# Delta rule of a hybrid decoder step: substitution, decays, samples' norm and late reciprocals in another order, with products of ones in the first group

## What is computed

```python
diff = gam[..., :, None] - gam[..., None, :]          # gam: cumulated gates
decay = where(incl, exp(diff), 0)
a_mat = where(strict, beta * (k @ k.T) * decay, 0)
tinv = triangular_solve(eye + a_mat, eye)             # inverse of a unit lower triangle
value = tinv @ (v * beta);  kcum = tinv @ (k * beta * exp(gam))
qk = (q @ k.T) * decay
# over the chunks, with state s:
u = value - kcum @ s
o = (q * exp(gam)) @ s + qk @ u
s = s * exp(gam_last) + (k * exp(gam_last - gam)).T @ u
# then
o = o * rsqrt(mean(o * o) + eps) * norm_w * silu(z)   # z: a projection of the layer's input
```

## Time and profile before

| | |
|---|---|
| median of 3 runs | 2327.48 us (2322.49 to 2330.67) |
| profiled execution | 2326.65 us, span 2324.8 us |
| TensorE busy, mean granted clock | 2173.9 us (94%), 0.969 |
| VectorE, ScalarE, GpSimd busy | 1005.6, 577.4, 1123.5 us |
| delta rule stage | 1238 to 1748 us of the span |

### The profile page before, as it was taken

The page is one execution under the profiler, slowest core; times in us unless marked ns, Lnnn a source line. Parts: engine busy times, 40 slices in busy tenths (PEclk is TensorE's granted clock), DMA queues, the critical chain, the costliest instruction groups (busy, mean ns, idle before and its releaser), DMA issues. The chain is left out here.

```text
span 2324.8 us, 33108 instructions
## 1 busy us (share of the span) xinstructions
PE 2173.9 (94%) x12562; PEld 1621.2 (70%) x12562; DVE 1005.6 (43%) x1879; ACT 577.4 (25%) x1292; POOL 1123.5 (48%) x1075
## 2 busy tenths in 40 slices
PE   9898999899999999899996798888899999999997
PEld 6675555477777777677775667675767767777776
DVE  5343675435411341467884634343443163313422
ACT  2103677410000000155553324242420010000011
POOL 3212555357653564565783524334227276644653
PEclk9999999999999999999997899989999999999998
DMA  9725002722222211512223223242303122122211
GB/s 330 221 81 179 1 2 84 285 73 73 73 73 89 75 55 74 195 55 70 71 76 80 55 63 120 50 131 55 123 24 131 73 89 74 55 75 107 73 73 41
DMA packets 125911, 216.46 MB, mean 93 GB/s; under 512 B 73602, under 2 KB 96002, under 8 KB 109762
## 3 DMA queue, kind: packets, MB, share of 16 engines
q1 hardware_dynamic: 119234, 197.13, 25.5%
q0 software_dynamic: 3088, 14.03, 1.8%
q10 hardware_dynamic: 3440, 3.25, 0.4%
HBM read 185.08 MB, written 37.55 MB: 96 GB/s over the span
## 5 line engine op out<-in xcount | busy, mean ns | idle before, releaser
L2014 PE MATMUL ps<-xn,ring 128*128 128x288 f32 x768 | 198.8, 407 | 5.4 <-DVE xn L2117 3.2
L2014 PE MATMUL ps<-hid,ring 128*128 128x288 f32 x768 | 192.8, 406 | 0.0
L2014 PEld LDWEIGHTS ps<-xn,ring 128*128 128x128 f32 x768 | 145.3, 190 | 48.3 <-DVE xn L2117 5.9
L2014 PEld LDWEIGHTS ps<-hid,ring 128*128 128x128 f32 x768 | 145.6, 190 | 40.7 <-ACT p L2051 0.8
L2097 POOL TENSOR_TENSOR prod<-prod,rstd 128x1152 f32<-128x1152 f32 x32 | 84.0, 2623 | 179.5 <-DVE prod L2181 163.2
L2051 ACT ACTIVATE p<-ps 128x288 f32<-128x288 f32 x48 | 19.7, 411 | 597.4 <-PE ps L2014 597.4
L3725 PE MATMUL ps<-xn,ring 128*128 128x288 f32 x512 | 146.3, 425 | 5.7 <-PE ps L3823 4.0
L2014 PE MATMUL ps<-x_sum,wsum 128*128 128x288 f32 x512 | 130.6, 407 | 3.4 <-DVE x_sum L2121 1.9
L1122 POOL TENSOR_SCALAR ring<-ring,fac 128x128 f32<-128x128 f32 (+2 forms) x96 | 92.4, 980 | 83.1 <-DVE fac L1551 83.1
L2071 POOL TENSOR_TENSOR wsum<-ring 128x512 f32<-128x512 f32 x64 | 81.9, 1280 | 99.4 <-DMA ring<-in_w_mlp 91.5
L2014 PE MATMUL ps<-hid_sum,wsum 128*128 128x288 f32 x512 | 128.4, 407 | 0.1
(11 more groups left out here) (597 smaller groups left out, 4643.7 us busy)
## 6 DMA issues: line engine op xcount, KB each, us to landing
ring<-in_w_mlp SPq DMA_DIRECT2D x64, 1024.0 KB, 4.8
ring<-in_w_gdn_in SPq DMA_DIRECT2D x16, 1024.0 KB, 4.9
ring<-in_w_nsa_in SPq DMA_DIRECT2D x9, 1024.0 KB, 17.5
ring<-in_w_gdn_z SPq DMA_DIRECT2D x8, 1024.0 KB, 5.2
x<-in_seq_state SPq DMA_DIRECT2D x4, 2048.0 KB
out_seq_state<-x SPq DMA_DIRECT2D x4, 2048.0 KB, 11.6
ring<-in_w_gdn_out SPq DMA_DIRECT2D x8, 1024.0 KB, 5.6
out_win_old<-in_win_rows POOLq DMA_DIRECT2D x1, 8064.0 KB, 46.5
```

The lines of the kernel that those rows point to most:

```text
L2014: mm = nc.tensor.matmul(S.ps[:, base + BANK[p], 0:HT], stationary(p, blk.units[pair // 4], pair % 4), moving(blk.kind, p, pair), start=pai ...
```

## The change

- **VectorE**: chunks 12 and 13 get their unit length before the first keys step of group 0; 15 stays behind tile 2; 14 goes into the samples' part of group 0. The samples' norm of each group is made in its own samples' part.
- **ScalarE**: in group 0, decay 1 follows values and keys of tile 0. In other groups the decays of tiles 0 and 1 are made at the end of the group before, as are the square, root and output of the samples' norm.
- **GpSimd**: three of the eight scalings of the projection's input go before the first gaps, five behind the first two tiles. The samples' front goes before the substitution. The gaps and grown keys of the next group's tiles 1 and 0 go between the substitution and the scaling of the states.
- **TensorE**: in group 0, products of ones (128 x 512 outputs, `keep_busy`) where later groups have fillers: 6, 2, 1, 1 and one behind each of the last four steps of the first `join`, fourteen by the code. The key products for the next group's inverses go behind the value product of tile 0. The samples' norm is turned in its own group. One filler of the samples' front moves one step later.
- **SP**: the next group's rows and grown rows are loaded before the inverses are stored, its inverses after the ring load; the key products are stored after the loads for tile 3.
- The substitution's working tiles go from `root2` to `rstd` (free once 13 is made), gates to `shared`, keys to a free part of a tile in set 1.

```diff
-LATE_AT = {(0, -1): 12, (0, 0): 13, (0, 1): 14, (0, 2): 15}
+LATE_ORDER = (12, 13, 15, 14)
...
-        place = BlockPlace(S.root2[:, 0:256], S.root2[:, 256:512], S.root2[:, 512:576], S.rstd[:, 0, 0:32], S.rstd[:, 0, 32:288])
+        place = BlockPlace(S.rstd[:, 0, 0:256], S.rstd[:, 0, 256:512], S.rstd[:, 0, 512:576],
+                           S.shared[:, SMALL_AT + 24:SMALL_AT + 56], wide[1]["t"][:, 256:512])
...
                 if hg < 3:
+                    nxt = [tile(hg + 1, i) for i in range(2)]
+                    wait_step(sp, C[1], "pe", w[3].job, "out")
+                    rows_load(nxt[1])
+                    grown_load(nxt[1])
+                    wait_step(sp, Q, "pe", hg, "p4")
+                    rows_load(nxt[0])
...
                     block_inverses_out(sp, blocks, place, hg + 1)
                 sp.wait_ge(zd.product, 4 * hg + 2)
...
+                ring_load(2 * hg + 4)
+                if hg < 3:
+                    sp.wait_ge(blocks.stored, 256 * (hg + 2))
+                    wait_step(sp, Q, "pe", hg, "value")
+                    for x in nxt:
+                        t_load(x)
+                        inverse_load(x)
...
+            scaled(0, 3)
+            for i in range(2):
+                decay_gaps(tile(0, i))
+                grown_keys(tile(0, i))
+            scaled(3, KD)
...
                 seq_rows(hg)
+                seq_front(hg)
                 for _ in substitution:
                     pass
-                seq_front(hg)
+                if hg < 3:
+                    for i in (1, 0):
+                        decay_gaps(tile(hg + 1, i))
+                        grown_keys(tile(hg + 1, i))
                 wait_step(pool, Q, "pe", hg, "value")
...
+                def pause(n, ones):
+                    if hg:
+                        fill(n, left)
+                    else:
+                        keep_busy(S, ones, 7)
+
                 first_products(first)
-                fill(1, left)
+                pause(1, 6)
                 keys_turned(first)
-                fill(2, left)
+                pause(2, 2)
                 joins = join(first)
                 next(joins)
-                fill(1, left)
+                pause(1, 1)
                 first_products(second)
                 next(joins)
                 keys_turned(second)
-                fill(1, left)
+                pause(1, 1)
                 for _ in joins:
-                    fill(1, left)
+                    pause(1, 1)
...
+                    if i == 0 and hg < 3:
+                        pe.wait_ge(z_out, 4 * hg)
...
-                    fill((1, 3, 0, 1, 1, 1, 1, 1)[k])
+                    fill((1, 2, 1, 1, 1, 1, 1, 1)[k])
...
                 pe.sem_inc(Q.sem["pe"], 1)
+                turn(NQ, 0, hg)
                 fill(2)
...
-                decay(w[0])
-                decay(w[1])
+                if hg == 0:
+                    decay(w[0])
                 values(w[0])
                 late_keys(w[0])
+                if hg == 0:
+                    decay(w[1])
                 values(w[1])
-                if hg:
-                    square(*norm_of(hg, -1), hg - 1, PT)
...
+                square(*norm_of(hg, PT), hg, PT)
+                root(*norm_of(hg, PT))
+                if hg < 3:
+                    for i in (1, 0):
+                        decay(tile(hg + 1, i))
+                silu_z(hg, 1)
+                out(*norm_of(hg, PT), hg, PT)
+                silu_z(hg, 2)
...
+                if hg == 0:
+                    unit_length(12)
+                    unit_length(13)
                 keys(w[0])
...
                 by_sequence(0)
+                if hg == 0:
+                    unit_length(14)
+                last = norm_sum(*norm_of(hg, PT))
+                next(last)
                 for j in range(4):
                     if j < 3:
                         by_sequence(j + 1)
+                    if j == 1:
+                        next(last)
```

More of the change, by code:

```diff
@@ L3328, in _ @@
                 else:
[L3329 to L3337, removed]
                     sp.wait_ge(zd.product, 4 * hg)
-                    unit = 2 * hg + 3
-                    nxt, unit = (zd, unit) if unit < 8 else (out_d, unit - 8)
-                    sp.dma_start(S.ring[:, unit % SLOTS], nxt.weights[unit]).then_inc(nxt.loaded[unit % SLOTS], 16)
+                    ring_load(2 * hg + 3)
                     sp.wait_ge(seq_add, hg * 8)
@@ L3459, in _, with scaled @@
                 pool.sem_inc(c.sem["pool"], len(c.order["pool"]))
[L3460 to L3463, removed]
+            def scaled(first, last):
+                for k in range(first, last):
+                    g.tensor_tensor(S.xn[:, k], S.xn[:, k], S.rstd[:, 1], ALU.mult).then_inc(xn_ready, 1)
+            scaled(0, 3)
[3 more added lines that the diff above has]
+            scaled(3, KD)
             g.memset(zm, 0.0).then_inc(zm_zero, 1)
@@ L3466, in _ @@
                 substitution = block_inverses(pool, S, place, hg + 1) if hg < 3 else iter(())
-                decay_gaps(tile(hg, 2))
-                grown_keys(tile(hg, 2))
-                if hg == 0:
-                    for k in range(KD):
-                        g.tensor_tensor(S.xn[:, k], S.xn[:, k], S.rstd[:, 1], ALU.mult).then_inc(xn_ready, 1)
-                decay_gaps(tile(hg, 3))
-                grown_keys(tile(hg, 3))
+                for i in range(2, 4):
+                    decay_gaps(tile(hg, i))
+                    grown_keys(tile(hg, i))
                 if hg:
@@ L3485, in _ @@
                     g.tensor_tensor(seq_state[:, j], seq_state[:, j], seq_total(S, hg, j), ALU.mult).then_inc(seq_decayed, 1)
-                if hg < 3:
-                    for i in range(2):
-                        decay_gaps(tile(hg + 1, i))
-                        grown_keys(tile(hg + 1, i))
             last_gate()
@@ L3933, in _ @@
                 for i in range(PT):
-                    last = norm_before(hg, i)
+                    last = norm_before(hg, i) if i else None
                     if w[i + 1]:
@@ L3946, in _ @@
                     if last:
[L3947 removed]
+                        out(*last, hg, i - 1)
                     if w[i + 1]:
@@ L3972, in _ @@
                 act.sem_inc(Q.sem["act"], 1)
-                if hg == 3:
-                    square(*norm_of(3, PT), 3, PT)
-                    root(*norm_of(3, PT))
-                for c in range(1, 4 if hg == 3 else 3):
-                    if c == 3:
-                        out(*norm_of(3, PT), 3, PT)
-                    silu_z(hg, c)
+                square(*norm_of(hg, PT), hg, PT)
[6 more added lines that the diff above has]
+                silu_z(hg, 2)
+                if hg == 3:
+                    silu_z(hg, 3)
         @block.vector
@@ L4172, in _ @@
                 by_sequence(0)
-                last = norm_sum(*norm_of(3, PT)) if hg == 3 else iter(())
-                next(last, None)
+                if hg == 0:
+                    unit_length(14)
+                last = norm_sum(*norm_of(hg, PT))
+                next(last)
                 for j in range(4):
@@ L4183, in _ @@
                                         ALU.add).then_inc(seq_add, 1)
-                for _ in last:
-                    pass
 def gdn_out_stage(S, block):
```

46 lines of the change are left out of this document (18 added, 28 removed).

## The result

The changed kernel takes **2309.35 us** (median of 5 runs, 2303.71 to 2311.1) against 2323.77 us of the kernel before on the same chip (5 runs, 2322.49 to 2330.67): a ratio of 0.9928, with a 95% interval of 0.9906 to 0.995. It is faster, by 14 us where 37 were forecast. The profiled execution took 2311.1 us (span 2309.4, mean granted clock 0.974).

The account below looks back on a forecast made before the run. TensorE's instruction order, its waits for other engines' order and low clock behind them bound the stage; group 0 -15.5, groups 1 and 2 -9.1 each, group 3 -3.6, together -37.3 us, gave 2290 us, range 2278 to 2309.

Parts of the forecast that it names:

- Reciprocals 13 and 14 leave the loop: Group 0's tile loop: TensorE's waits of 4.79 and 4.09 us and the low clock behind them go, 12.5 us gained.
- Substitution behind the samples' front: Samples' part of groups 1 and 2: the 4.18 us wait for GpSimd goes and the clock recovers, 7.0 us each.
- A filler moved: Samples' part of all four groups: a filler set in a 0.51 us wait gives 0.5 us each.
- Start of group 0: Earlier values and keys steps, and products of ones holding the clock, gain 4 us; bounds +1 and -6.
- Reciprocal 14: Samples' part of group 0: 4.5 us on VectorE costs nothing, covered by GpSimd's delay; without cover some 2 us, once.
- GpSimd late: Samples' part of groups 0 to 2: GpSimd's later state scalings delay the second update product, +1.5 us each.
- Group starts: Groups 1 to 3: moved norm, earlier decays and recovered clock save 3.1 us per group.
- the 3.44 us wait: Group 0's tile loop: the wait for reciprocal 15, kept in tile 2, stays as the one such wait left.
- the wait of 4.18 us: Samples' part of groups 1 and 2: TensorE's wait for GpSimd, still in the substitution, would be gone.
- The clock gives nothing back: Rival, chance 0.18: remaining waits keep TensorE's clock low, some 18 us of gain is missing, 2308 us.
- GpSimd bounds the samples' part: Rival, chance 0.12: VectorE holds up GpSimd's instructions, whose chain ends 6 us later in three groups, 2308 us.
- More comes back: Rival, chance 0.10: the clock holds through the start and all group starts, some 8 us more, 2282 us.

Follow-up runs that it names:

- e7: Changed kernel with the four late reciprocals (12 to 15) back where they were before the change; 2313.49 us, 0.9951 of the kernel before.
- e5: Changed kernel with GpSimd making the samples' front behind the substitution again; 2321.06 us, 0.9977 of the kernel before.
- e6: Changed kernel with all eight gate input scalings on GpSimd behind the first two tiles' gaps and grown keys; 2304.68 us, 0.9915 of the kernel before.
- e8: Changed kernel with tile 2's rows before weights and states, state scalings before next gaps, reciprocal 14 after group 0's last state addition, gate inputs scaled late; 2273.66 us.
- e1: Changed kernel without its fourteen products of ones in group 0's start; 2307.16 us, 0.9915 of the kernel before.
- e2: Changed kernel with reciprocal 14 behind group 0's last state addition instead of before the second spread; 2301.66 us, 0.9884 of the kernel before.
- e4: Changed kernel with GpSimd scaling the samples' states ahead of the next group's gaps and grown keys; 2300.72 us, 0.989 of the kernel before.
- e3: Changed kernel with SP issuing tile 2's rows and ready inverses before the weights and sample states; 2286.44 us, 0.9822 of the kernel before.
- e9: Kernel before, with only tile 2's rows issued by SP before the weights and states; 2311.94 us, 0.9935 of the kernel before.
- e10: Changed kernel with early tile 2 rows, early state scalings, late reciprocal 14 and late gate input scalings, but no products of ones; 2278.97 us, 0.978.

## Why the prediction was wrong

The direction and most of the mechanism were right, the size was not: 2290 forecast, 2309 measured, 0.35 us beyond the range. By its steps:

- *Reciprocals 13 and 14 leave the loop*, -12.5: right; -15.5 measured, of which 12.2 by e7. Waits and clock both came back.
- *Substitution behind the samples' front*, -7.0: right, -6.9 and -7.0 by e5. *A filler moved*, -0.5: -0.4 in group 3.
- *Start of group 0*, -4: **failed**, +0.3. The step that failed is "the keys step ends at 1247.9, the first inverse product can start at 1248.0", 9.9 us after the stage's start; it started 12.1 after. It priced each late chunk at 4.5 us, from a trace in which nothing of GpSimd ran beside the multiply, though the change puts GpSimd's scalings there: the two chunks took 10.9 us, not 9. The products behind the wait then ran at the low clock. e6 has a start 3.5 us shorter, e8 2.3. I had cited the rule of the shared port (the Trainium skill, SBUF — State Buffer) against the change, but charged it only in the samples' part; by the rows 1.62 and 1.84 us beside GpSimd against 1.00 and 0.76, that rule and the trace agree here too. The ones were worth 0.9 us in the start and 3.2 in the group by e1, at twice the price assumed for one.
- *Reciprocal 14*, nothing, "GpSimd's delay covers it; without cover some 2 us": **failed**, 4.5 by e2. It ends, multiply and all, at 1349.5, and behind it stand two steps of the norm and a spread of 2.35 us before the first addition. I had moved one instruction and not the queue behind it; the clock then doubled the price.
- *GpSimd late*, +1.5: the mechanism was right. In group 0 it measured 1.6 (e8 against e2), in groups 1 and 2 3.1 and 3.0 (e4), because there the wait of 0.9 us was followed by a filler at the low clock.
- *Group starts*, -3.1 each: **failed**, and for more than the lost 4.6 us. The step was "the product runs in the wait and the following one waits instead: I take 1.2 us". It put the 2.94 us down to the norm's place in ScalarE's order and counted the late rows as something unmoved, when it was the rows that ended last: their distance from the group's start is the same 29.9 us, so nearly nothing could be gained in front of them: the wait that I had put at 1.2 us is 4.9, 5.6 and 5.3. The clock of 0.64 behind it stayed too (L3576 took 1.02 us against 0.67 in e3). e3 and e9 show it.

Of the misses, 4.3 us are the start, 4.8 the samples' part of group 0, 3.6 those of groups 1 and 2, 4.6 the group starts, 1.8 the norm's turn, which moved from the next group's loop to behind the last update; the loop gave 3.0 more than forecast. That is 16.1 of the 16.2 us between -37.3 and -21.1.

Of the signs named, the 3.44 us wait stayed in the loop, the wait of 4.18 us was gone, and a new wait stood before the second update; but group 0 was not some 120 us long, and the samples' part took 45.8, 42.7, 42.7 and 39.6 us, not 41.

Two rivals named 2308 and so came nearest. "The clock gives nothing back" did so for another reason than the true one: the clock did come back where the waits went (group 0 from 0.83 to 0.93). "GpSimd bounds the samples' part" was true in small: 1.6 us in group 0 and 3 in groups 1 and 2, not 6 in three. "More comes back" (2282) did not come true either: e3 comes near its number (2286) because a wait went. No wait of TensorE was for a load of inverses, and the 0.95 for faster was justified.

Open: what the attention part's clock depends on, the gap of 2.5 us of e10, why a filler behind a wait of 0.9 us ran at the low clock in some executions and not in others, and the 2.06 us for the copy at L3864, which stayed in every kernel with the change. None was tried. Nor were the moves at the group starts (the norm, the decays a group ahead, the block keys, SP's order) undone one by one, so their -0.8, -2.7 and -1.2 us are shown as a sum only.

## What to carry to other kernels

When a wait is put down to a copy on an in-order engine, ask what that engine itself was waiting for just before; if that is a load, look at what stands ahead of the load in its queue before you rearrange any compute. Here the place of two loads in one queue gave 21 us, and 16 in the kernel before, three quarters of what all the moves of the change gave. When an instruction is moved onto an engine with slack, price it with its neighbours: what stands behind it on the queue, and the other engine that will be running beside it.

## What the runs showed that was not expected

- The clock was low behind a wait of only 0.89 us between two updates: the filler behind it took 3.76 us in place of 2.18, with a clock of 0.76 in the window from 1475 to 1482 us:

```profile
1475.00:1482.00 7.00, 6.41 (x17) 3.33 (x16) 5.63 (x8) 0.00 (x0) 4.85 (x3) 0.76 0.79 254
```

  Before the wait TensorE had run two 32-row update products and four filler products (four and eight records), with pauses of 0.19 us. Wait and clock together cost 3.1 us. It is no rule: behind 0.93 us in e6 the same filler took 2.18, with a clock of 1.00.
- A float32 product of 128 x 512 leaves two records of 0.44 to 0.46 us in the trace, so twelve in a row are six products.
- VectorE's product of two SBUF inputs, 128 x 576, took 0.76 us alone and 1.62 to 1.84 beside GpSimd's scalings or grown keys.
- 256 KB of rows took 13.0 us behind 3 MB of the same queue and 3.3 us ahead of them, while the 3 MB behind cost nothing that could be seen.
